# A two-layer encoder kernel: the second layer's latent blocks 2 and 3 are requested without waiting for the last scatter

## What is computed

```python
for l in range(DEPTH):                       # DEPTH = 2
    xn = rms_norm(x, norm_mix[l])
    c_q, c_kv, k_rope, dq, dk, dv, mu, mv, mo, mg = jnp.split(xn @ w_in[l], split_at, axis=-1)
    ...
    x = x + jnp.concatenate([y_mla, y_dil, y_ml], axis=-1) @ w_out[l]
    x = x + hier_moe(rms_norm(x, norm_ffn[l]), ...)   # 16 experts, top 2 of one group
```

## Time and profile before

| | us |
|---|---|
| median of 3 runs | 1827.36 (1826.84 to 1828.09) |
| the profiled execution's own time | 1829.1 |
| its span from the first instruction to the last | 1827.3 |
| PE busy in the span | 1815.0 (99%) |
| layer boundary: `c0` starts on PE | 917.1 |
| SP issues `c0` / `c1`, `c2` of the second layer | 883.3 to 890.2 / 910.0 to 911.3 |

### The profile page before, as it was taken

The page is one execution under the profiler, slowest core; times in us unless marked ns, Lnnn a source line. Parts: engine busy times, 40 slices in busy tenths (PEclk is TensorE's granted clock), DMA queues, the critical chain, the costliest instruction groups (busy, mean ns, idle before and its releaser), DMA issues.

```text
span 1827.3 us, 28277 instructions
## 1 busy us (share of the span) xinstructions
PE 1815.0 (99%) x12238; PEld 1376.1 (75%) x12238; DVE 737.0 (40%) x1531; ACT 313.7 (17%) x846; POOL 13.8 (1%) x27
## 2 busy tenths in 40 slices
PE   9999999999999999999999999999999999999999
PEld 8788888899765667656597888878996666666665
DVE  3477665676202121121235675656761021221123
ACT  3022222211201111011021231232121111110010
POOL 1000000000000000000000000000000000000000
PEclk9999999999999999999999999999999999999999
DMA  9443443437999999999884343443579999999997
GB/s 375 150 164 116 172 167 133 173 140 292 376 425 424 427 428 426 427 427 422 358 341 156 126 184 112 160 189 118 213 290 364 426 420 428 426 428 427 428 421 293
DMA packets 51150, 546.90 MB, mean 299 GB/s; under 512 B 5840, under 2 KB 6224, under 8 KB 13776
## 3 DMA queue, kind: packets, MB, share of 16 engines
q1 hardware_dynamic: 48528, 531.47, 71.0%
q0 software_dynamic: 2496, 13.57, 2.0%
HBM read 540.78 MB, written 4.24 MB: 298 GB/s over the span
## 4 chain that ended last, share of the span: by engine, by line
PE 96%; DMA 2%; SPq 1%; DVE 0%; issue 0%; ACT 0%; DVEq 0%
PE ps L855 93%; DMA ring<-in_moe_w_down 1%; PE ps L909 1%; SPq L753 1%; PE ps L1328 0%; DMA ring<-in_w_lat 0%; PE ps L925 0%; PE ps L917 0%; PE ps L1215 0%; PE ps L1387 0%; PE ps L1008 0%; DVE ring L1924 0%; PE ps L1096 0%; PE ps L1123 0%; PE ps L1162 0%
## 5 line engine op out<-in xcount | busy, mean ns | idle before, releaser
L855 PE MATMUL ps<-ring,scr 128*64 128x256 f32 (+2 forms) x3488 | 624.7, 423 | 0.9 <-issue 0.5
L855 PEld LDWEIGHTS ps<-ring,scr 128*64 128x64 f32 (+1 forms) x3488 | 337.5, 138 | 213.1 <-issue 120.6
L855 PE MATMUL ps<-ring,XN 128*128 128x256 f32 (+2 forms) x1184 | 244.4, 363 | 2.8 <-DMA ring<-in_w_lat 2.7
L855 PEld LDWEIGHTS ps<-ring,XN 128*128 128x128 f32 x1184 | 212.3, 191 | 23.8 <-DMA ring<-in_w_lat 3.3
L855 PE MATMUL ps<-ring,X 128*128 128x256 f32 x896 | 200.6, 379 | 0.0
L855 PE MATMUL ps<-XN,ring 128*128 128x128 f32 (+1 forms) x1312 | 195.8, 306 | 0.0
L855 PEld LDWEIGHTS ps<-XN,ring 128*128 128x128 f32 x1312 | 180.2, 191 | 12.7 <-issue 3.1
L855 PEld LDWEIGHTS ps<-ring,X 128*128 128x128 f32 x896 | 169.6, 190 | 22.7
L855 PE MATMUL ps<-PR,scr 128*64 128x256 f32 (+2 forms) x704 | 173.8, 402 | 0.0
L2199 DVE TENSOR_TENSOR v_mla<-scr,ps 128x256 f32<-128x256 f32 x32 | 13.5, 421 | 390.6 <-PE ps L855 390.6
L855 PE MATMUL ps<-BIAS,scr 128*64 128x256 f32 (+1 forms) x576 | 149.4, 416 | 0.0
(11 more groups left out here) (278 smaller groups left out, 1456.7 us busy)
## 6 DMA issues: line engine op xcount, KB each, us to landing
ring<-in_moe_w_gate SPq DMA_DIRECT2D x38, 2048.0 KB, 21.1
ring<-in_w_main SPq DMA_DIRECT2D x36, 2048.0 KB, 9.5
ring<-in_moe_w_down SPq DMA_DIRECT2D x32, 2048.0 KB, 22.7
ring<-in_moe_w_up SPq DMA_DIRECT2D x30, 2048.0 KB, 17.8
ring<-in_w_out_a SPq DMA_DIRECT2D x16, 1280.0 KB, 5.8
PR<-in_moe_w_up SPq DMA_DIRECT2D x10, 2048.0 KB, 16.7
XN<-in_moe_w_down SPq DMA_DIRECT2D x10, 2048.0 KB, 20.2
ring<-in_moe_w_up SPq DMA_DIRECT2D x20, 1024.0 KB, 21.7
```

What stands on the lines that cost most here:

```text
L855: return pe.matmul(o, lhsT, rhs, start=start, stop=stop, skip_group_check=True)
```

## The change

The two lines of the wait are moved behind the two loads. `c1` and `c2` then wait for their own slots alone, and `up` takes over the wait for `sc0` in addition to its own.

```diff
@@ -704,10 +704,10 @@
                         load_x(q)
                     sp.dma_start(slot("c0")[:, q * part:(q + 1) * part], a["w_lat0"][l][:, q * part:(q + 1) * part]).then_inc(
                         c0_in[q] if q < 3 else slot_full[SLOTS.where("c0")], 16)
+                for j in (1, 2):
+                    load(f"c{j}", l, a["w_lat12"][l, j - 1], width=KT * LAT[j][1])
                 if l:
                     sp.wait_ge(*ready(f"sc0_{NE // 2 - 1}", l - 1))
-                for j in (1, 2):
-                    load(f"c{j}", l, a["w_lat12"][l, j - 1], width=KT * LAT[j][1])
 
                 load("up", l, a["w_up"][l], width=3 * W_D + 1024)
```

## The result

The changed kernel takes 1831.59 us (median of 13 runs, 1830.4 to 1836.14); the kernel before takes 1828.09 us in the same comparison (13 runs, 1825.25 to 1829.9). The ratio is 1.0023, with a 95% interval of 1.0015 to 1.003. So it is slower by 3.5 us (by the medians) to 4.2 us (by the ratio). The interval lies above 1, so the loss is real, and it is about as large as the 0.2%, or 3.65 us, that the prediction had set as the bound of what counts as a change. The prediction said 1827.7 within 1826.3 to 1829.2, and no change.

What follows compares the result with a forecast made beforehand. The prediction took PE, busy 99% of the span, as the bound; its terms, 0 + 0 + 0.14 + 0.22 = +0.36 us on 1827.36, gave 1827.7 us, within 1826.3 to 1829.2, called no change.

Steps and rivals of the forecast that it cites:

- Term 1: Earlier landing of `c1` and `c2`: PE waits for neither block, so it saves 0 us.
- Term 2: Last down half, ahead of `c1` on SP's queue: not delayed, 0 us, with 3.5 us as upper bound.
- Term 3: PE's instruction fetch at line 1422's branch: two packets wait 0.22 us each, adding +0.14 and +0.22 us.
- The cover of 0.08 us: At line 1422's branch: already queued matmuls hide 0.08 us of the first instruction packet's delay.
- Rival 1: At the branch, fetches wait for a whole batch of eight packets: +3.5 us, 1830.9, at most 1834.5; chance 0.07.

Runs made afterwards that it cites:

- e6: The changed kernel with PE's branch of line 1422 and its body left out in both layers; ratio 0.9989 to the kernel before.
- e12: The changed kernel, but SP first waits for the last down product of round 7 before requesting `c1` and `c2`; ratio 0.9998 to the kernel before.
- e1: The changed kernel with only `c1` ahead of the wait and `c2` behind it, as before; ratio 1.0018 to the kernel before.
- e8: The changed kernel with eight jumped-over matmuls added at the top of the branch's body in the first layer; ratio 1.0018 to the kernel before.
- e7: The kernel before with eight jumped-over matmuls added at the top of the branch's body in the first layer; ratio 0.9998 to the kernel before.
- e4: The kernel before with `mu0` requested right behind `c0`, while `c1` and `c2` stay behind the wait; ratio 1.002 to the kernel before.
- e3: The changed kernel with each latent block requested in four quarters, in rows of 2,944 bytes; ratio 1.0025 to the kernel before.
- e10: The changed kernel with eleven matmuls of a constant, results unread, put before the branch in the first layer; ratio 1.0044 to the kernel before.
- e2: The changed kernel with only `c2` ahead of the wait and `c1` behind it; ratio 1.0015 to the kernel before.

## Why the prediction was wrong

**The place was right, the size was not.** The prediction put the whole cost on the instruction packets of line 1422's branch, on two of them, and on nothing else. e6 shows that this is the place. The prediction gave them +0.36 us; they cost 4.55 us in the profile and 3.5 to 4.2 us in the times.

**Term 1 (0 us for the earlier landing)** held. `c1` landed at 888.8 + 22.4 = 911.2 and `c2` at 899.8 + 14.8 = 914.6. After the scatter none of the changed kernel's rows up to `mu0` has a wait for a weight.

**Term 2 (0 us for the downs)** held. The last half lands 29.9 us after its issue in the changed kernel, as before. The gap of 0.60 us at 903.81 has nothing to do with `c1`: PE was earlier there, not the weight later. e12, which asks for nothing before the downs are done, has such a gap too (0.24 us), and e1 with `c1` early has none.

**Term 3 failed**, in the step "Each queue gives up the engine after one packet. So a fetch waits for one packet at most". The first half of it is what the earlier trace rows show, for two queues that both have work all the time. The second half doesn't follow. It sized each wait at 0.22 us and 0.45 at most. The first packet started 2.4 us later than before (3.4 against 1.0), which became the gap of 2.53 us, and the second 1.5 us later (2.8 against 1.3), which made its part of the scatter 1.9 us longer; together that is 4.4 of the 4.55 us. A queue that comes newly with its first packet waited here as if the engine had already taken on some work from the other; how it does so the profile doesn't show. The same trace could have told. POOL issues the write of X at 919.32; the queues of the kernel before in 919.3 to 923.9 are these, without a queue 0 among them:

```profile
q1 hardware_dynamic: 126, 1.57, 100.3%
q8 instruction: 1, 0.02, 1.3%
```

4.6 us after its issue the write had not begun. In the first layer POOL issues a load at 49.51, with SP's queue running dry, and in 49.5 to 51.9 queue 0 is already at work:

```profile
q0 software_dynamic: 15, 0.07, 27.9%
q1 hardware_dynamic: 9, 0.08, 8.1%
```

Its first packet starts at 51.3, 1.8 us after the issue. The difference of some 2.9 us between the two is of the size of what the instruction packet had to wait: 3.4 - 1.0 = 2.4 us in the changed kernel. It is a rough guide, since one is a write and the other a load. I read rows from the middle of the transfer and should have read its beginning. The cover of 0.08 us was right: the branch got longer by 2.60 us, and the gap is 2.53.

**What was missing** besides is the clock. A gap of 2.53 us was followed by some 3.4 us at half clock in the changed kernel. No step had it, since no step had a gap. In the profiled execution it cost nothing of its own, because the wait for the second packet lay over it; where that wait is short or absent, it costs up to 1.6 us (e8 against e7). The other executions, which have no profile, suggest that it happens in most of them. The granted clock of a whole execution is 0.9975 in the mean over the changed kernel's 13 runs, 0.9975 over e1's and 0.9976 over e4's, and 0.9984 over the 35 runs of the kernel before in the comparison of e1 and e4. A fall of 3.4 us to half is 0.5 x 3.4 / 1828 = 0.0009 of it. So by estimate all three have about one fall more per execution than the kernel before, e1 and e4 too, whose profiled executions happened to have none here. Falls elsewhere, as the one at 1366.2, make part of the spread: seven of those 35 runs have a clock of 1.000 and take 1826.2 us in the mean, three have 0.996 and take 1831.0.

**Rival 1** came out in sign and size (1830.9 against 1831.6, and waits of 2.4 and 1.5 us against its 1.8 and 1.8), with a chance of 0.07. That was too low: its ground against was the reading above, and for it spoke that two uncovered waits lay where the load was moved to. By the prediction's own test (a branch of 5 us or more) the profile points to this rival. Its mechanism, as written, does not hold quite: the wait isn't a batch of the eight packets of one block. With quarters (e3) eight rows are 0.9 us at most, and the wait was 2.3 us. With `mu0` (e4) they are up to 4.9 us, and the wait of 2.6 us tells nothing. The Trainium skill (DMA: Bandwidth & Descriptors, Queues, rings and completion order) states a change of ring after some 9 to 17 descriptors. No run here bears out a count: rows from 2,944 to 16,384 bytes gave nearly the same wait, some 20 rows in e3 and some 6 in e10 by the estimates above. It does agree in that the wait is far more than one packet.

## What to carry to other kernels

Before a load is moved into a quiet stretch of the DMA engines, look at what else uses them there: a taken branch on the critical engine waits for its own instruction packet, and part of what is queued then goes in front of it, here 2.3 to 2.8 us of an engine's work. In the changed kernel some 2.4 us in front of one 16 KB packet cost more than any slack in the weights could give, while the weights had 10 us of slack and needed nothing. When you want to know how long a newcomer waits on a busy DMA engine, read the time from issue to first packet of a queue that starts under load, not how two running queues share.

A version clearly better than the kernel before and with the branch in it was not found (e12's five short executions are unexplained); the branch itself is worth 1.2 us of the stretch (11.79 to 10.60).

## What the runs showed of the hardware

- A newly requested instruction packet starts 0.8 to 1.5 us after the branch when little is queued (1.0 in the kernel before), and 3.3 to 3.8 us after it when a whole block or more is queued on SP's queue, with rows of 2.9 to 16 KB alike. A half block gave 1.7 us.
- The branch ended 1.4 to 1.9 us after its packet did, in twelve profiles.
- Two queues that both have work share the engines about evenly and in short turns: in 926 to 932 of the kernel before queue 1 starts 79 packets and queue 0 starts 78, some five of each on an engine. A queue's first packet under load is another matter: POOL's write of X began 4.6 us after its issue.
- The packet's landing place in the code matters: 32 records of padding in a body that is never run took away a pause of 1.08 us (e7).
- Around the end of PE gaps of 2.5 to 4.3 us the granted clock fell to 0.5 for some 3.4 us in the profiles of the changed kernel, e2, e3, e8 and e10, and in e12 after a pause of 3.5 us. In e1 and e4, with gaps of 2.8 and 2.7 us, it did not in the profiled execution. What decides it is open. It cost 1.6 us in e8, where PE had no other wait, and nothing in the changed kernel, where PE waited for a packet anyway.
